# The recurrent mixers: mask inside the minimum, q and k decayed in place, half of each score tile copied, row broadcasts in fp32r parts

## The chip, the cores and the metric

The kernel runs on one core of a Trainium2 chip. The metric is the device time of one execution in microseconds (us), the median of several runs.

## The reference

Two blocks of transformer-like layers run one after the other over 256 tokens of width 1024, in fp32. The first has four layers, each a mixer and a SwiGLU feed-forward with layer norms: gated DeltaNet (gdn), hgrn2, gla, gated DeltaNet again. The second has two layers ("four") with four small mixers side by side. The change concerns the causal part of three mixers:

```python
def chunk_gla(q, k, v, g):            # hgrn2 (8 heads of 128) and gla (4 heads of 128 keys, 256 values)
    G = jnp.cumsum(g, axis=-2)        # g <= 0, one decay per token and key channel
    rel = jnp.exp(jnp.where(incl, G_c[..., :, None, :] - G_c[..., None, :, :], -jnp.inf))
    a = jnp.einsum('bhcd,bhsd,bhcsd->bhcs', q_c, k_c, rel)
    ...
def chunk_gated_delta_rule(q, k, v, beta, g):   # gdn, 8 heads
    decay = jnp.exp(jnp.where(incl, G[..., :, None] - G[..., None, :], -jnp.inf))
    L = jnp.where(strict, jnp.einsum('bhncd,bhnsd->bhncs', kb, k) * decay, 0.0)
    sol = lax.linalg.triangular_solve(L + jnp.eye(CHUNK, dtype=F32), rhs, ...)
    a_qk = jnp.einsum('bhncd,bhnsd->bhncs', q, k) * decay
    ...
```

The Mamba-like mixer of the "four" layers masks its decay in the same way: `where(tri, exp(where(tri, seg, 0)), 0)`.

## The kernel before, in words

Five engines run programs of their own and meet at semaphores. The weights stream from HBM into a ring of six slots; DVE or ACT casts a slot to its fp32r high part (`w_hi`), DVE and POOL subtract it from the slot to get the low part (`w_lo`), and PE multiplies high by high, high by low and low by high. `units_in(kind)` lists the slots of a mixer's input projection. In the projection of hgrn and gla, DVE's `split` of the next slots is placed by hand between the mixer's own vector work, by calls of `due(n)`.

**hgrn and gla** (`gla` on each engine). The 256 tokens are halved again and again: at level `lv` a block of `2 << lv` tokens has a first half (keys) and a second half (queries). For each of eight levels POOL subtracts from the cumulated log decay its value at the block's middle (`differences`, L1361), ACT takes the exponential of both halves, DVE multiplies k and q by it into a fresh copy (`decayed`, L1888 `inv<-yb,ct` and `inv<-pj,ct`), PE multiplies all tokens of each 128-token tile with each other (L980, or L988 for the last level), and DVE copies what the level's mask selects into the score matrix `at`, which lies in the tile `mats` (`masked`, COPY_PREDICATED, L2358). PE also runs filler matmuls (`stay_awake`, L574) at levels 0 and 1. Then PE multiplies the scores with the values (L818, L819).

**gdn**. For each of eight heads PE broadcasts the two rows (cumulated decay and beta) over the partitions (L849, `ident` against `rows`, fp32), DVE forms the clipped difference in `dec` (L1894) and `kbeta`, ACT takes the exponential, POOL multiplies by the causal mask `incl` (L1396), and DVE multiplies both score tiles by it (`scores`, `mats<-bank,dec`). Then a triangular inverse is built by doubling, over six levels and four groups of matrices: POOL masks (L1402), DVE takes identity minus that (`XT` of level 0, `inv<-ident,ct`), PE transposes (L923), forms `cx` (L867) and corrects (L935, at level 6 L937), ACT copies `cx` and transposes out of PSUM, DVE subtracts.

**four**. DVE forms the same clipped difference for four heads, ACT the exponential, DVE multiplies by `incl` and then by the scores (L1888); the rotation of q and k stands behind it on DVE.

## Time and profile before

| what | value |
|---|---|
| median of 3 runs | 2405.71 us (2405.37 to 2406.33) |
| the profiled execution's own time | 2406.07 us |
| its span in the trace | 2404.4 us |
| PE, DVE, ACT, POOL busy | 94%, 65%, 38%, 20% of the span |
| mean granted TensorE clock | 0.959 of full speed |

Times in the trace are counted from the span's start. The span leaves 1.7 us of the execution's time outside. The recurrent mixers stand at about 125 to 235 us (gdn), 555 to 617 (hgrn), 923 to 962 (gla) and 1295 to 1405 (gdn again); the "four" mixers lie behind 1620.

### The profile page before, as it was taken

Reading aid. Unit: us, or ns where it says so; the run is one execution under the profiler, and the core shown is the slowest. Engines: PE = TensorE matmul, PEld = TensorE weight load, DVE = VectorE, ACT = ScalarE, POOL = GpSimd, SP = SyncE. Lnnn points to the kernel's source line nnn. Section 1 sums busy time; section 2 is a strip of 40 time slices with the busy share of each in tenths; the row PEclk is TensorE's granted clock in tenths of the full one; section 3 lists DMA queues with packets and bytes.
Section 4 is the critical chain, followed back from the end, with each engine's and each line's share of the span. In section 5 each row is a group of like instructions: output and inputs, shape, how many; then the busy total and the mean of one; then the engine's idle time right before and its main releaser. Section 6 shows DMA issues by size and latency. Waiting matters only on the chain.

```text
span 2404.4 us, 33475 instructions
## 1 busy us (share of the span) xinstructions
PE 2261.9 (94%) x13233; PEld 1949.9 (81%) x13233; DVE 1572.1 (65%) x1914; ACT 902.7 (38%) x1193; POOL 469.1 (20%) x259
## 2 busy tenths in 40 slices
PE   8999999997999988999899999998889999978999
PEld 7988788887788778788798878877658997847998
DVE  7843754798854567844695275456467887457787
ACT  3324344333344413444413334442453333254332
POOL 6643000156000044000063500004120001320000
PEclk9989999999999999999999899999879999969999
DMA  7500565551265542565462026555204554503552
GB/s 219 163 31 19 175 193 187 165 181 46 98 216 184 170 142 86 176 192 185 132 187 94 1 88 219 185 159 160 72 27 165 181 188 131 166 0 100 190 187 94
DMA packets 265598, 333.69 MB, mean 139 GB/s; under 512 B 16492, under 2 KB 228593, under 8 KB 265473
## 3 DMA queue, kind: packets, MB, share of 16 engines
q1 hardware_dynamic: 265473, 331.93, 43.1%
q8 instruction: 90, 1.47, 0.3%
q14 instruction: 35, 0.29, 0.0%
HBM read 330.84 MB, written 1.05 MB: 138 GB/s over the span
## 4 chain that ended last, share of the span: by engine, by line
PE 82%; DVE 10%; ACT 4%; issue 3%; POOL 2%; DVEq 0%; POOLq 0%; ACTq 0%
PE bank L530 41%; PE bank L502 26%; DVE inv L1888 3%; PE bank L867 2%; PE bank L935 2%; PE bank L574 1%; PE bank L564 1%; DVE w_hi L1932 1%; ACT stat L1409 1%; PE bank L923 1%; DVE mats L2358 1%; PE bank L721 1%; PE bank L849 1%; PE bank L1070 1%; ACT xh L1409 1%
## 5 line engine op out<-in xcount | busy, mean ns | idle before, releaser
L1934 DVE TENSOR_TENSOR w_lo<-ring,w_hi 128x2048 fp32r<-128x2048 f32 (+3 forms) x297 | 562.0, 1894 | 328.6 <-ACT w_hi L1455 325.4
L1455 ACT ACTIVATE w_hi<-ring 128x2048 fp32r<-128x2048 f32 x204 | 385.5, 1890 | 463.6 <-PE bank L530 299.2
L1350 POOL TENSOR_TENSOR w_lo<-ring,w_hi 128x1536 fp32r<-128x1536 f32 (+3 forms) x71 | 277.0, 3902 | 1402.3 <-DVE w_hi L1932 1402.3
L530 PE MATMUL bank<-w_lo,xh 128*128 128x512 f32 x992 | 268.2, 392 | 4.2 <-POOL w_lo L1350 4.2
L530 PE MATMUL bank<-w_hi,xh 128*128 128x512 f32 x928 | 251.1, 392 | 11.9 <-ACT xh L1409 7.4
L502 PE MATMUL bank<-xh,w_lo 128*128 128x256 f32 (+2 forms) x1880 | 246.3, 284 | 4.8 <-POOL w_lo L1350 4.7
L530 PE MATMUL bank<-w_hi,xl 128*128 128x512 f32 x928 | 249.0, 390 | 0.0
L502 PE MATMUL bank<-xh,w_hi 128*128 128x256 f32 (+1 forms) x1816 | 242.0, 287 | 4.3 <-DVE w_hi L1932 4.3
L502 PEld LDWEIGHTS bank<-xh,w_lo 128*128 128x128 f32 (+2 forms) x1880 | 232.1, 188 | 8.0 <-issue 5.6
L502 PEld LDWEIGHTS bank<-xh,w_hi 128*128 128x128 f32 (+1 forms) x1816 | 229.3, 192 | 11.3 <-issue 6.5
L502 PE MATMUL bank<-xl,w_hi 128*128 128x256 f32 (+1 forms) x1816 | 236.4, 283 | 0.0
L502 PEld LDWEIGHTS bank<-xl,w_hi 128*128 128x128 f32 (+1 forms) x1816 | 224.9, 190 | 0.7
L530 PEld LDWEIGHTS bank<-w_lo,xh 128*128 128x128 f32 x992 | 185.5, 189 | 43.6 <-issue 6.1
L530 PEld LDWEIGHTS bank<-w_hi,xh 128*128 128x128 f32 x928 | 173.1, 188 | 51.5 <-issue 11.6
L530 PEld LDWEIGHTS bank<-w_hi,xl 128*128 128x128 f32 x928 | 174.8, 188 | 36.8
L1932 DVE CAST w_hi<-ring 128x2048 fp32r<-128x2048 f32 (+2 forms) x93 | 171.0, 1839 | 43.2 <-PE bank L502 23.4
L530 PE MATMUL bank<-w_hi,hid_hi 128*128 128x512 f32 x528 | 169.0, 401 | 8.1 <-DVE hid_lo L1888 8.1
L530 PE MATMUL bank<-w_hi,hid_lo 128*128 128x512 f32 x528 | 165.1, 394 | 0.0
L530 PE MATMUL bank<-w_lo,hid_hi 128*128 128x512 f32 x528 | 164.3, 393 | 0.0
L1409 ACT ACTIVATE yb<-bank 128x256 f32<-128x256 f32 (+3 forms) x146 | 59.0, 404 | 171.4 <-PE bank L530 124.9
L530 PEld LDWEIGHTS bank<-w_lo,hid_hi 128*128 128x128 f32 x528 | 100.2, 190 | 21.9
L530 PEld LDWEIGHTS bank<-w_hi,hid_lo 128*128 128x128 f32 x528 | 100.1, 190 | 21.9
(300 smaller groups left out, 2801.4 us busy)
## 6 DMA issues: line engine op xcount, KB each, us to landing
ring<-in_ffn_w_in_dram SPq DMA_DIRECT2D x264, 512.0 KB, 4.5
ring<-in_ffn_w_down_dram SPq DMA_DIRECT2D x88, 512.0 KB, 4.3
ring<-in_gdn_w_in_dram SPq DMA_DIRECT2D x64, 512.0 KB, 5.1
ring<-in_ffn_w_out_dram SPq DMA_DIRECT2D x44, 512.0 KB, 4.1
ring<-in_w_in_dram SPq DMA_DIRECT2D x36, 512.0 KB, 4.6
ring<-in_hgrn_w_in_dram SPq DMA_DIRECT2D x32, 512.0 KB, 4.6
...
```

The lines of the kernel that those rows point to most:

```text
L502: m = nc.tensor.matmul(cols, *((wk, xk) if tokens == ALL else (xk, wk)), start=(first and step == 0 and k == 0 and (j % 2 == 0)), stop=(la ...
L530: m = nc.tensor.matmul(bank[:, 0:width], xin[:, k0 + k, rows_of], w[:, k, c * width:(c + 1) * width], start=(first and step == 0 and k == ...
L564: m = nc.tensor.transpose(b[:, j * P:(j + 1) * P], src[:, t, c * CHUNK + j * P:c * CHUNK + (j + 1) * P], ident[:, :])
L574: m = nc.tensor.matmul(b[:, 0:T], ones[:, :], incl[:, 0:T], start=True, stop=True)
L867: m = nc.tensor.matmul(b[:, (j % 4) * HALF2:(j % 4 + 1) * HALF2].rearrange("p (n c) -> p n c", c=1 << lv), ct[:, j, :], first_halves(inv[: ...
L935: m = nc.tensor.matmul(b[:, cols], inv[:, 16 + j, :], cx[:, j, :], start=True, stop=True)
L1350: g.tensor_tensor(w_lo[:, unit % RING, part], ring[:, unit % RING, part], high_part(unit)[:, part], ALU.subtract).then_inc(*pool_lo.tick())
L1409: nc.scalar.activation(out_, in_, func, **kw).then_inc(*sig.tick(*key))
L1455: nc.scalar.activation(high_part(u)[:, 0:n], ring[:, u % RING, 0:n], ACT.Copy).then_inc(*act_hi.tick())
L1888: v.tensor_tensor(out_, a, b, op).then_inc(*sig.tick(*key))
L1932: v.tensor_copy(high[:, 0:n], w[:, 0:n]).then_inc(*dve_hi.tick())
L1934: v.tensor_tensor(w_lo[:, u % RING, 0:share], w[:, 0:share], high[:, 0:share], ALU.subtract).then_inc(*dve_lo.tick())
```

## The change

In hgrn and gla the running sum of log decays, POOL's differences and ACT's exponentials go away. The decay itself (`ratio`) is multiplied up pairwise into the decay of blocks of 2, 4, ... tokens (`block_ratio`). q is multiplied once by the decay of its own token (`qd`, which lies in `sq`), and from level to level k and `qd` are multiplied in place: only the half of each block that moves on is touched (`grown`), half of the heads at a time. The masked copy touches only the second half of each block's columns, 64 of each 128. The scores lie in `own` (two 128-token squares for each head) and `across` (the first against the second 128 tokens). The last of the eight levels is a plain copy. The fillers at levels 0 and 1 and the clearing of `at` are dropped. hgrn's scale of q moves into the later norm, and its log of the bounded forget gate is formed as `sigma * (1 - lb) + lb`.

In gdn and four the mask lies in the minimum (`imask` holds 0 or -1e30), so the multiplications by `incl` go. The rows to be broadcast are split into fp32r high and low parts, one matmul of 512 columns for each. The level-0 groups of gdn's inverse are taken in the order 0, 2, 1, 3, the first two between the last heads' scores. At level 6 `cx` is formed for the 64 rows and columns that are not zero. The core of the diff, without the setup of masks and the changed ACT code of the forget gate:

```diff
-                    for j in range(2):
-                        m = nc.tensor.matmul(b[:, j * T:(j + 1) * T], ident[0:8, h:h + 1].to_broadcast([8, P]), rows[0:8, j, :], start=True, stop=True)
+                    for n, part in enumerate((rows_hi, rows_lo)):
+                        m = nc.tensor.matmul(b[:, :], pick[0:8, h:h + 1].to_broadcast([8, P]),
+                                             part[0:8, :, :].rearrange("p a n -> p (a n)"), start=(n == 0), stop=(n == 1))
                     m.then_inc(*pe_gdn.tick("bcast", layer, h))
...
-                for g in range(4):
+                for g in (0, 2, 1, 3):
...
-                            m = nc.tensor.matmul(b[:, (j % 4) * HALF2:(j % 4 + 1) * HALF2].rearrange("p (n c) -> p n c", c=1 << lv),
-                                                 ct[:, j, :], first_halves(inv[:, j, :], lv), start=True, stop=True)
+                            cols_of = slice((j % 4) * HALF2, (j % 4 + 1) * HALF2)
+                            if lv < 6:
+                                m = nc.tensor.matmul(b[:, cols_of].rearrange("p (n c) -> p n c", c=1 << lv),
+                                                     ct[:, j, :], first_halves(inv[:, j, :], lv), start=True, stop=True)
+                            else:
+                                m = nc.tensor.matmul(b[HALF2:HALF, cols_of], ct[0:HALF2, j, HALF2:HALF], inv[0:HALF2, j, 0:HALF2],
+                                                     start=True, stop=True)
...
+                        m = nc.tensor.matmul(b[0:HALF2, cols], cx[HALF2:HALF, j, :], inv[HALF2:HALF, 16 + j, HALF2:HALF], start=True, stop=True)
                 m.then_inc(*pe_gdn.tick("z", layer, lv, g))
...
+                pe.wait_ge(*dve_gla.at("q decayed", layer))
+                for lv in range(8):
+                    for g in range(2):
+                        if lv:
+                            pe.wait_ge(*dve_gla.at("grown", layer, lv - 1, g))
+                        if lv == 7:
+                            b = psum.claim(pe, "level", layer, lv, g)
+                            for j in range(heads // 2):
+                                h = g * heads // 2 + j
+                                m = nc.tensor.matmul(b[:, j * P:(j + 1) * P], k[:, h, 0:HALF], qd[:, h, HALF:T],
+                                                     start=True, stop=True)
+                            m.then_inc(*pe_gla.tick("level", layer, lv, g))
+                            continue
+                        for n in range(heads // 4):
+                            b = psum.claim(pe, "level", layer, lv, g, n)
+                            for j in range(4):
+                                h, t = g * heads // 2 + 2 * n + j // 2, slice((j % 2) * HALF, (j % 2 + 1) * HALF)
+                                m = nc.tensor.matmul(b[:, j * P:(j + 1) * P], k[:, h, t], qd[:, h, t], start=True, stop=True)
+                            m.then_inc(*pe_gla.tick("level", layer, lv, g, n))
...
-                    pe.wait_ge(*dve_gla.at("causal", layer))
+                    pe.wait_ge(*dve_gla.at("causal", layer, g // 2))
...
-                for h in range(8):
-                    pool.wait_ge(*act_gdn.at("decay", layer, h))
-                    d = dec[:, h % 2, :]
-                    g.tensor_tensor(d, d, incl[:, :], ALU.mult).then_inc(*pool_gdn.tick("decay", layer, h))
                 for lv in range(7):
...
-                    dve.wait_ge(*pool_gdn.at("decay", layer, h))
+                    dve.wait_ge(*act_gdn.at("decay", layer, h))
...
+                def first_inverse(g):
+                    dve.wait_ge(*pool_gdn.at("masked", layer, 0, g))
+                    tt(s, inv[:, 16 + 4 * g:16 + 4 * g + 4, :], ident[:, :].rearrange("p (a n) -> p a n", a=1).to_broadcast([P, 4, P]),
+                       ct[:, 4 * g:4 * g + 4, :], ALU.subtract, "XT", layer, 0, g)
...
-                    ts(s, dec[:, h % 2, 0:T], b[:, 0:T], cols[:, 0, h:h + 1], ALU.subtract, 0.0, ALU.min)
-                    ts(s, dec[:, h % 2, T:TRI], b[:, HALF:T], cols[:, 2, h:h + 1], ALU.subtract, 0.0, ALU.min,
-                       "difference", layer, h)
+                    stt(s, dec[:, h % 2, 0:T], b[:, 0:T], cols[:, 0, h:h + 1], imask[:, 0:T], ALU.subtract, ALU.min)
+                    stt(s, dec[:, h % 2, T:TRI], b[:, HALF:T], cols[:, 2, h:h + 1], imask[:, T:TRI], ALU.subtract, ALU.min,
+                        "difference", layer, h)
                     tt(s, sq[:, h, :], pj[:, 8 + h, :], b[:, T:2 * T], ALU.mult, "kbeta", layer, h)
                     psum.release(s, "bcast", layer, h)
                     if h:
                         scores(h - 1)
+                    if h >= 6:
...
-                    dve.wait_ge(*pool_gdn.at("masked", layer, 0, g))
-                    tt(s, inv[:, 16 + 4 * g:16 + 4 * g + 4, :], ident[:, :].rearrange("p (a n) -> p a n", a=1).to_broadcast([P, 4, P]),
-                       ct[:, 4 * g:4 * g + 4, :], ALU.subtract, "XT", layer, 0, g)
+                for g in (1, 3):
+                    first_inverse(g)
...
+                    tt(s, flat(ct), ratio, f, ALU.subtract, "log k", layer)
+                    due(2)
+                    dve.wait_ge(*s.now())
+                    dve.wait_ge(*act_gla.at("sigma", layer))
                     for h in range(8):
-                        ts(s, sq[:, h, :], decayed_sum[:, h * T:(h + 1) * T], lbs[:, 5, h:h + 1], ALU.add, lbs[:, 4, h:h + 1], ALU.subtract,
-                           "f against bound", layer)
-                    due()
+                        ts(s, ratio[:, h * T:(h + 1) * T], sq[:, h, :], lbs[:, 5, h:h + 1], ALU.mult, lbs[:, 4, h:h + 1], ALU.add)
+                dve.wait_ge(*act_gla.at("sigma", layer))
+                dve.wait_ge(*act_gla.at("k", layer))
+                due()
+                for lv in range(6):
+                    w = block_ratio(lv, heads)
                     dve.wait_ge(*s.now())
-                    for h in range(8):
-                        ts(s, decayed_sum[:, h * T:(h + 1) * T], decayed_sum[:, h * T:(h + 1) * T], lbs[:, 5, h:h + 1], ALU.add, lbs[:, 4, h:h + 1], ALU.max)
-                    due(2)
...
-                dve.wait_ge(*s.now())
-                for h in range(heads):
-                    scan(s, pj[:, 8 + h, :], decayed_sum[:, h * T:(h + 1) * T], "cumulated", layer)
-                    if h == 3:
+                    tt(s, block_ratio(lv + 1, heads).rearrange("p h n two -> p h (n two)"), w[:, :, :, 0], w[:, :, :, 1], ALU.mult)
+                    if lv < 2:
                         due()
-                due(2)
                 dve.wait_ge(*act_proj.at("q", layer, 6 if kind == "hgrn" else 2))
-                if kind == "hgrn":
-                    ts(s, flat(q), flat(q), 128.0 ** -0.5, ALU.mult)
-                s.name_also("qk", layer)
+                tt(s, flat(qd)[:, 0:n], flat(q), ratio[:, 0:n], ALU.mult, "q decayed", layer)
...
+                def grown(lv, g):
+                    of, w = slice(g * hg, (g + 1) * hg), block_ratio(lv, heads)
+                    if lv < 6:
+                        kg, qg, wk, wq = kk[:, of, :], qd[:, of, :], w[:, of, :, 1], w[:, of, :, 0]
+                    else:
+                        kg, qg, wk, wq = kk[:, of, 0:HALF], qd[:, of, HALF:T], w[:, of, 0:1, 1], w[:, of, 1:2, 0]
+                    for x, by, which in ((kg, wk, 0), (qg, wq, 1)):
+                        x = halves(x, lv, which)
+                        tt(s, x, x, by.rearrange("p h (n a) -> p h n a", a=1).to_broadcast(list(x.shape)), ALU.mult, "grown", layer, lv, g)
...
+                def masked(lv, g):
+                    c = 1 << lv
+                    m = halves(level[:, lv:lv + 1, :].bitcast(U32), lv, 1).to_broadcast([P, 4, HALF2 // c, c])
+                    for n in range(hg // 2):
+                        h0 = g * hg + 2 * n
+                        to = own[:, h0:h0 + 2, :, :].rearrange("p h t n -> p (h t) n")
+                        scores = psum.bank("level", layer, lv, g, n)[:, :].rearrange("p (a n) -> p a n", a=4)
+                        v.copy_predicated(halves(to, lv, 1), m, halves(scores, lv, 1)).then_inc(*s.tick("masked", layer, lv, g))
+                        psum.release(s, "level", layer, lv, g, n)
...
+                for lv in range(7):
+                    for g in range(2):
+                        dve.wait_ge(*pe_gla.at("level", layer, lv, g, hg // 2 - 1))
+                        if lv:
+                            dve.wait_ge(*s.at("masked", layer, lv - 1, g))
+                        else:
+                            dve.wait_ge(*s.now())
+                        grown(lv, g)
+                        masked(lv, g)
...
+                        stt(s, at[:, h, 0:T], b[:, j * T:(j + 1) * T], cols[:, 0, h:h + 1], imask[:, 0:T], ALU.subtract, ALU.min)
+                        stt(s, at[:, h, T:TRI], b[:, j * T + HALF:(j + 1) * T], cols[:, 2, h:h + 1], imask[:, T:TRI], ALU.subtract, ALU.min,
+                            "difference", layer, h)
...
-                    tt(s, at[:, h, :], at[:, h, :], incl[:, :], ALU.mult)
-                    dve.wait_ge(*s.now())
                     tt(s, at2[:, 4 + h, :], psum.bank("bc", layer, h // 2)[:, 0:TRI], at[:, h, :], ALU.mult, "causal", layer, 3)
```

**DVE in hgrn's levels, before.** `inv` takes k (`yb`) and q (`pj`) times the decays (`ct` or `sq`); `mats` is the score tile. Levels 0 and 1:

```order
L1888 TENSOR_TENSOR inv<-yb,ct 128x1024
L1888 TENSOR_TENSOR inv<-pj,ct 128x1024
L2369 MEMSET mats 128x3072
L2358 COPY_PREDICATED mats<-ident,bank 128x2x2x128 x4
L1888 TENSOR_TENSOR inv<-yb,sq 128x512x2
L1888 TENSOR_TENSOR inv<-pj,sq 128x512x2
L2358 COPY_PREDICATED mats<-level,bank 128x2x2x128 x4
```

**The same place after.** `yb` is k and `sq` is the decayed q, both in place; `inv` holds the block decays; the second `yb`, `sq` pair is the other half of the heads at level 0:

```order
L1887 TENSOR_TENSOR mats<-bank,ident 128x512 x4
L1887 TENSOR_TENSOR yb<-yb,inv 128x512
L1887 TENSOR_TENSOR sq<-sq,inv 128x512
L2360 COPY_PREDICATED mats<-level,bank 128x256 x2
L1887 TENSOR_TENSOR yb<-yb,inv 128x512
L1887 TENSOR_TENSOR sq<-sq,inv 128x512
L2360 COPY_PREDICATED mats<-level,bank 128x256 x2
```

The long multiplications have become twice as many of half the length, into their own operand; each masked copy moves 256 elements in a partition in place of 512, and the memset is gone.

**DVE at the end of gdn's scores, before** (`mats` are the two score tiles, `inv<-ident,ct` the level-0 inverses):

```order
L1894 TENSOR_SCALAR dec<-bank,cols 128x256
L1894 TENSOR_SCALAR dec<-bank,cols 128x128
L1888 TENSOR_TENSOR sq<-pj,bank 128x256
L1888 TENSOR_TENSOR mats<-bank,dec 128x384 x2
L1894 TENSOR_SCALAR dec<-bank,cols 128x256
L1894 TENSOR_SCALAR dec<-bank,cols 128x128
L1888 TENSOR_TENSOR sq<-pj,bank 128x256
L1888 TENSOR_TENSOR mats<-bank,dec 128x384 x4
L1888 TENSOR_TENSOR inv<-ident,ct 128x512 x4
```

**After:**

```order
L1897 SCALAR_TENSOR_TENSOR dec<-bank,cols,imask 128x256
L1897 SCALAR_TENSOR_TENSOR dec<-bank,cols,imask 128x128
L1887 TENSOR_TENSOR sq<-pj,bank 128x256
L1887 TENSOR_TENSOR mats<-bank,dec 128x384 x2
L1887 TENSOR_TENSOR inv<-ident,ct 128x512
L1897 SCALAR_TENSOR_TENSOR dec<-bank,cols,imask 128x256
L1897 SCALAR_TENSOR_TENSOR dec<-bank,cols,imask 128x128
L1887 TENSOR_TENSOR sq<-pj,bank 128x256
L1887 TENSOR_TENSOR mats<-bank,dec 128x384 x2
L1887 TENSOR_TENSOR inv<-ident,ct 128x512
L1887 TENSOR_TENSOR mats<-bank,dec 128x384 x2
L1887 TENSOR_TENSOR inv<-ident,ct 128x512 x2
```

Two of the four level-0 inverses have moved ahead of the last heads' scores.

**DVE in hgrn's projection, from the log decay on, before** (each CAST with its `w_lo` is one slot of weights):

```order
L1932 CAST w_hi<-ring 128x2048
L1934 TENSOR_TENSOR w_lo<-ring,w_hi 128x512
L1932 CAST w_hi<-ring 128x2048
L1934 TENSOR_TENSOR w_lo<-ring,w_hi 128x512
L1888 TENSOR_TENSOR inv<-inv,ct 128x2048
L1903 SCALAR_TENSOR_TENSOR pj<-const,inv 128x256 x4
L1932 CAST w_hi<-ring 128x2048
L1934 TENSOR_TENSOR w_lo<-ring,w_hi 128x512
L1903 SCALAR_TENSOR_TENSOR pj<-const,inv 128x256 x4
L1932 CAST w_hi<-ring 128x2048
L1934 TENSOR_TENSOR w_lo<-ring,w_hi 128x512
L1892 TENSOR_SCALAR pj<-pj 128x2048
```

**After:**

```order
L1887 TENSOR_TENSOR ct<-inv 128x1024
L1931 CAST w_hi<-ring 128x2048
L1933 TENSOR_TENSOR w_lo<-ring,w_hi 128x512
L1887 TENSOR_TENSOR ct<-ct 128x512
L1931 CAST w_hi<-ring 128x2048
L1933 TENSOR_TENSOR w_lo<-ring,w_hi 128x512
L1887 TENSOR_TENSOR ct<-ct 128x256
L1887 TENSOR_TENSOR ct<-ct 128x128
L1887 TENSOR_TENSOR ct<-ct 128x64
L1887 TENSOR_TENSOR ct<-ct 128x32
L1887 TENSOR_TENSOR sq<-pj,inv 128x2048
L1931 CAST w_hi<-ring 128x2048
```

Eight of the sixteen multiplications by the bounds (ahead of these rows), the eight scans, the add and the scaling of q are gone; short products of decays and one long product (`sq<-pj,inv`) stand ahead of the last slot's cast.

## Rows read from the trace of the kernel before

**Rows 1.** The page: busy time, share of the span and instructions of each engine

```profile
PE 2261.9 (94%) x13233; PEld 1949.9 (81%) x13233; DVE 1572.1 (65%) x1914; ACT 902.7 (38%) x1193; POOL 469.1 (20%) x259
```

**Rows 2.** Stretch of hgrn's levels: busy PE, PEld, DVE, ACT, POOL; granted clock; DMA

```profile
559.70:609.70 50.00, 37.49 (x260) 35.18 (x258) 49.14 (x52) 14.23 (x14) 23.31 (x7) 0.90 0.01 2
```

**Rows 3.** Timeline of DVE, hgrn's last levels: start, duration, operation, count

```profile
597.76 2.27 DVE L1888 TENSOR_TENSOR inv<-yb,ct 128x1024 f32<-128x1024 f32 x1
601.20 2.55 DVE L2358 COPY_PREDICATED mats<-level,bank 128x512 f32<-128x512 uint32 x4
603.66 1.20 DVE L1888 TENSOR_TENSOR inv<-yb,sq 128x1024 f32<-128x1024 f32 x1
```

**Rows 4.** Timeline of PE, hgrn: scores of one pass, values

```profile
554.90 3.74 PE L980 MATMUL bank<-pj,yb 128*128 128x128 f32 x32
609.91 0.67 PE L818 MATMUL bank<-mats,vb 128*128 128x256 f32 x2 [1.50 <-DVE mats L2374]
```

**Rows 5.** Timeline of gla: PE's first scores and values, DVE's last level

```profile
922.74 1.95 PE L980 MATMUL bank<-pj 128*128 128x128 f32 x16
950.43 1.28 DVE L1888 TENSOR_TENSOR inv<-pj,sq 128x512 f32<-128x512 f32 x2
953.80 0.67 PE L818 MATMUL bank<-mats,vb 128*128 128x256 f32 x2 [0.88 <-DVE mats L2374]
```

**Rows 6.** Timeline around the two projections' PE waits (idle time in brackets)

```profile
531.99 5.60 DVE L1888 TENSOR_TENSOR inv<-inv,ct 128x2048 f32<-128x2048 f32 x1
541.33 2.15 PE L502 MATMUL bank<-xh,w_hi 128*128 128x256 f32 x16 [3.02 <-DVE w_hi L1932]
895.96 1.17 PE L530 MATMUL bank<-w_lo,xh 128*128 128x512 f32 x4 [2.02 <-POOL w_lo L1350]
```

**Rows 7.** Timeline of one head of gdn's scores, PE and DVE

```profile
143.27 1.12 PE L849 MATMUL bank<-rows,ident 8*128 8x256 f32 x4
144.44 0.74 DVE L1894 TENSOR_SCALAR dec<-bank,cols 128x256 f32<-128x256 f32 x2 [0.50 <-PE bank L849]
145.42 1.08 DVE L1888 TENSOR_TENSOR mats<-bank,dec 128x384 f32<-128x384 f32 x2
145.83 1.12 PE L849 MATMUL bank<-rows,ident 8*128 8x256 f32 x4
```

**Rows 8.** Timeline from gdn's last scores to the first `cx`

```profile
151.90 14.10 POOL L1402 TENSOR_TENSOR ct<-mats,level 128x512 f32<-128x512 f32 x10
151.97 1.02 DVE L1888 TENSOR_TENSOR mats<-bank,dec 128x384 f32<-128x384 f32 x2 [0.35 <-POOL dec L1396]
153.21 6.76 DVE L1888 TENSOR_TENSOR inv<-ident,ct 128x512 f32<-128x512 f32 x4 [0.21 <-POOL ct L1402]
156.76 0.63 PE L923 MATMUL bank<-ident,inv 128*128 128x128 f32 x4 [1.05 <-DVE inv L1888]
161.00 3.51 PE L867 MATMUL bank<-inv,ct 128*128 128x64 f32 x16
```

**Rows 9.** Stretches of gdn's inverse: length, PE busy, granted clock

```profile
161.00:196.00 35.00, 34.67 (x241) 0.76 0.00 1
196.00:214.10 18.10, 17.77 (x161) 1.00 0.00 1
1330.50:1390.60 60.10, 59.45 (x466) 0.85 0.00 1
```

**Rows 10.** Timeline of PE in level 6: both matmul forms

```profile
216.05 0.68 PE L937 MATMUL bank<-inv,yb 128*64 128x64 f32 x8
216.66 1.10 PE L867 MATMUL bank<-inv,ct 128*128 128x64 f32 x8
```

**Rows 11.** The first "four" layer: DVE's mask multiplications, PE's wait, clock behind

```profile
1729.36 1.27 DVE L1888 TENSOR_TENSOR mats<-mats,incl 128x384 f32<-128x384 f32 x1
1738.24 0.76 PE L1092 MATMUL bank<-pj 64*128 64x128 f32 x2 [4.34 <-DVE pj L1888]
1734.30:1775.20 40.90, 28.43 (x71) 15.74 (x72) 22.79 (x54) 22.25 (x68) 13.05 (x12) 0.50 0.00 1
```

More of the change, by code:

```diff
@@ L51 @@
 CHAIN = [("gdn", 0), ("hgrn", 0), ("gla", 0), ("gdn", 1), ("four", 0), ("four", 1)]
-FILL = {"mixed": 9, "gdn": 5, "c2": 7, "kbeta": 5, "masked": 4, "level": 6, "softmax": 2}
+FILL = {"mixed": 9, "gdn": 5, "c2": 7, "kbeta": 5, "masked": 4, "softmax": 2}
 CHUNK = 4 * P
@@ L573, in stay_awake @@
                 for _ in range(n):
-                    m = nc.tensor.matmul(b[:, 0:T], ones[:, :], incl[:, 0:T], start=True, stop=True)
+                    m = nc.tensor.matmul(b[:, 0:T], ones[:, :], strict[:, 0:T], start=True, stop=True)
                 m.then_inc(*pe_filler.tick())
@@ L1311, in _ @@
                 fill(const[:, c:c + 1], v)
-            for ap in (blk64, incl, strict, later):
+            for ap in (blk64, strict, later):
                 fill(ap[:, :], 1.0)
-            for ap in (rot64, rot96, amask):
+            for ap in (rot64, rot96, amask, imask):
                 fill(ap[:, :], 0.0)
@@ L1725, in gla_decays @@
                     act.wait_ge(*dve_gla.at("bounds", layer))
-                    run(s, flat(lbs[:, 4:6]), flat(lbs[:, 4:6]), ACT.Ln, "log bounds", layer)
+                    run(s, lbs[:, 7, :], lbs[:, 7, :], ACT.Ln, "log bounds", layer)
                 else:
@@ L2363, in gla @@
[L2363 to L2377 removed]
+                hg = heads // 2
@@ new lines, in diagonal @@
+                def diagonal():
+                    m = ident[:, :].rearrange("p (a n) -> p a n", a=1).to_broadcast([P, 4, P])
+                    for g in range(hg):
+                        dve.wait_ge(*pe_gla.at("diagonal", layer, g))
+                        tt(s, own[:, 2 * g:2 * g + 2, :, :].rearrange("p h t n -> p (h t) n"),
+                           psum.bank("diagonal", layer, g)[:, :].rearrange("p (a n) -> p a n", a=4), m, ALU.mult, "diagonal", layer)
+                        psum.release(s, "diagonal", layer, g)
```

172 lines of the change are left out of this document (56 added, 116 removed).

## The prediction

> **What bounds the kernel now.** The page's first part says that PE is busy for 94% of the span [rows 1]. Most of that is fp32 projection and feed-forward work that the change does not touch. An edit to DVE, ACT or POOL can therefore pay only where PE waits for them or runs at the lower clock, so I read the mixers' stretches one by one, and in each what PE's next work waited for.
>
> In hgrn's levels the table of stretches shows DVE busy 49.14 of 50.0 us and PE 37.49 [rows 2]. A level takes DVE two long multiplications and four masked copies; from one to the next it is 603.66 less 597.76, 5.90 us [rows 3]. One level costs PE 3.74 us [rows 4]. So DVE sets the pace. The end of the projection is 554.8 us, where the first scores start, and the values start at 609.9: 55.1 us [rows 4]. gla is the same with half the heads: 922.7 to 953.8, 31.1 us [rows 5].
>
> In gdn's scores DVE waits 0.50 us for a broadcast in each head [rows 7] and PE is the pace. Behind the scores, POOL's masks (14.10/10 = 1.41 us each) and DVE's level-0 inverses (6.76/4 = 1.69 us each) go side by side, PE waits for each of them, and the first `cx` starts at 161.0 [rows 8]. From then on PE is busy nearly all the time, but at a mean granted clock of 0.76 until 196, that is partly at 1.2 in place of 2.4 GHz; the two levels from 196.0 to 214.1 ran at full clock, 18.1/2 = 9.05 us each [rows 9]. Before the clock fell PE had done short transposes with waits of about 1 us between them [rows 8].
>
> In "four" PE waits 4.34 us for DVE's rotation, which stands behind the mask multiplications [rows 11].
>
> **hgrn's levels.** The long multiplication took 2.27 us beside POOL and 1.20 alone [rows 3]; POOL has no work there any more. A multiplication of 512 elements, alone, is 1.28/2 = 0.64 us and steps at 0.655 [rows 5]. A masked copy of 512 steps at 2.55/4 = 0.64 [rows 3]. One of 256 has no row. From 1024 to 512 the multiplication fell by 1.20 - 0.64 = 0.56, or 1.1 ns an element, so 256 elements less are 0.27 and the copy is 0.38. The bounds are 0.32, half the old price, and 0.64, if strided reads save nothing. I take 0.38, since the strided multiplications before cost no more than others. A level is then 4 x 0.655 + 4 x 0.38 = 4.14 us. Six of them and the seventh with halved multiplications (4 x 0.39 + 4 x 0.38 = 3.1) are 27.9. PE's 3.74 fits beneath 4.14: one half of the heads costs it 1.87 us, while DVE has 2.8 us of other work before it needs the result. Ahead of that stand PE's diagonal scores (3.74) and the first half of level 0 (1.9), behind it one plain copy (0.65): the values start 34.5 us after the projection, not 55.1. **-20.6.** With copies at 0.64 it would be -13.3, with 0.32 -22.
>
> The Trainium skill, page "VectorE: DVE Perf Modes", section on the TRN2 errata, speaks against cutting operations in two: a fixed cost for each instruction, and (N + 151)/0.96 ns for an fp32 two-tensor operation. By it a level would be 4 x 0.69 + 4 x 0.42 = 4.44 us (an estimate), and hgrn's gain 2 us smaller. The row's 1.28 for two agrees with the single duration nearly, but successive operations overlap.
>
> **gla's levels.** A level is 4 multiplications of 256 (0.39) and 2 copies (0.38): 2.3 us; PE needs 1.95, its reply to one half 0.95 plus a hand-over of some 0.1 inside 1.5. Six, a seventh of 1.8, 3.0 ahead, 0.4 behind: the values start after 19.0 us in place of 31.1. **-12.1.** With copies at 0.64: -8.5.
>
> The fillers that go are 2.8 us of PE each, under DVE's time before. Their cover was for the clock; PE will be busy 90% (hgrn) and 80% (gla) of a level, against 3.74/5.9 = 63% before, so I cost their absence at nothing. If the cover is missed see the rivals.
>
> **The projections.** DVE's stretch in hgrn loses 8 bound multiplications, the 5.60 us addition [rows 6], scans and scaling, and gets products of under 3 us and one of 2048 elements (5.6 us beside POOL [rows 6], 2.3 alone). PE waits there three times, 6.2 us together, the longest 3.02 [rows 6]. Walking DVE's new order against PE's 5.8 us a slot, with a product held until POOL's current `w_lo` ends, the two waits in the middle go, and a wait of some 2.5 us stays before the last slot, whose cast stands behind the long product. **-3.8**, which is the 6.2 less the 2.5 that stays (from -1 to -7.7, where all PE idle goes, gaps between matmuls too). In gla a cast comes 1.7 us earlier and shortens PE's 2.02 us [rows 6]: **-1.7**; the larger wait ahead of it, for the gates, stays.
>
> **gdn, each of two.** (a) Broadcasts: PE's 1.06 us a head becomes two fp32r matmuls of 512 columns, of which the projection does four in 1.17 us [rows 6]: 0.6. The head then costs PE 2.0 and DVE about 2.2 (144.44 to 145.42 + 1.08, with what queues between heads) in place of the cadence 2.56 [rows 7]: 6 x 0.33 + 1.0 for the first two = 3.0; two inverses now stand in this stretch, +1.3; POOL's mask (0.35 on the last head [rows 8]) goes. -2.0. A subtraction with `imask` in place of 0 costs the same 0.74 for 384 elements. (b) Behind the last `lt` (152.5, the first of the two at 151.97 [rows 8]) `cx` came 8.5 us later. Now two POOL masks (2.8), an inverse (1.7) and a transpose (0.7) stand there: 5.4. -3.1. (c) Clock. The first three levels took 35.0 us; at the full clock's 9.05 they are 27.2 [rows 9]. PE's waits shrink to one of about 1 us, so I take it that the clock stays high: -7.8. (d) In level 6 the 64-wide form of 8 steps at 0.61 (216.05 to 216.66), the 128-wide at 1.03 [rows 10]: 4 x 0.42, of which 1.5 counts. Sum -14.4. The second gdn has the same rows to 0.1 us and a clock of 0.85 over its stage [rows 9]: **-28.8** for both.
>
> **four, each of two.** The first mask multiplication took 1.27 us, others 0.55 to 1.2, four of them some 3.3 us in steps [rows 11], all on the path to PE's wait of 4.34. **-3.3 each, -6.6.** Lower bound nothing, if POOL's rotation is late next; that ended ahead of DVE.
>
> The two-step split of gdn's rows adds 1 us of DVE at 40 us, where `rows` is not needed before 127. SP's queue keeps its order; no weight is waited for in these stretches.
>
> **Sum**: 20.6 + 12.1 + 3.8 + 1.7 + 28.8 + 6.6 = 73.6. The profiled execution took 2406.07 us (span 2404.4 and 1.7 around it), 0.4 above the median, so 2332.5, and 2332 against the median.
>
> **Rivals.**
> 1. The clock falls in gdn all the same, because PE's short waits remain (the transposes of groups 1 and 3) : +7.8 each, 2348. For it: the clock fell before on waits of only 1 us. Against: there were four of them in 8 us, now one. Chance 0.20.
> 2. The levels run slower than DVE's sum: copies at 0.64 give 7.3 + 3.6 = 11 us back, 2343; or PE, without fillers, falls to 1.2 GHz and needs 7.4 us a level in hgrn and 3.7 in gla, +22 and +10, 2364. Against the latter: 63% busy brought a mean clock of 0.90 [rows 2], no more. 0.12.
> 3. More is gained: all PE idle of hgrn's projection (4 us more), and in "four" the clock, which is 0.50 from 1734 to 1775 with PE 28.4 us busy [rows 11], comes back for part of it once the 4.34 us wait is gone. A third of the 28.4/2 us that it costs, twice, is 9: 2319. 0.13.
> 4. Slower than before. The in-place forms, with one decay repeated over a block and runs as short as one element, cost DVE more than any row here. The levels hold 56 + 42 = 98 such operations on the path. At 73.6/98 = 0.75 us more for each, above twice their price, the gain is gone; at 0.85 us more each it is 2332 + 98 x 0.85 = 2415. Against it: the level-0 operations of before stepped over two elements and cost the same 1.2. 0.03.
>
> Forecast 0.52, its own range 2323 to 2343. Less than 0.2% (4.8 us) either way is what a measurement of this kernel can't tell from no change. Faster 0.96, same 0.01, slower 0.03. The range takes in rivals 1 and 3 and the copies' bound: 2312 to 2356.
>
> **What would show it.** hgrn's values start about 34 us behind its last projection matmul, gla's 19; DVE without pause between them, masked copies near 0.4 us; PE's clock at full there. In gdn `cx` starts 5 to 6 us after the last `lt`, the clock stays high and the stage ends 14 us earlier. In "four" PE's wait is 1 us. Wrong would be: PE waits of over 1 us in each level, a clock of 0.5 behind gdn's scores, or copies of 0.6.

## The result, and the profile after

Medians of four executions each: 2405.77 us before (2405.37 to 2406.33), 2329.80 us after (2327.10 to 2331.76). The ratio is 0.9679, 95% interval 0.9664 to 0.9694: faster by 76 us, 3.2%. The forecast was 2332. The profiled execution took 2331.76 us (span 2330.1, mean clock 0.972).

The sum hit, but not each of its terms. Where the time went is read from PE's timeline. A stage lasts from PE's first matmul behind a mixer's input projection to the end of its last one ahead of the mixer's output projection. A gap is what lies between two stages: output projection, feed-forward and the next input projection, with PE's wait of 0.1 to 0.6 us just ahead of the output projection. Lengths in the two profiles, in us:

| stage or gap | before | after | difference | forecast |
|---|---|---|---|---|
| gdn, first | 114.7 | 99.0 | -15.7 | -14.4 |
| gap with hgrn's projection | 315.2 | 312.1 | -3.1 | -3.8 |
| hgrn | 68.4 | 47.5 | -20.9 | -20.6 |
| gap with gla's projection | 299.4 | 297.5 | -1.9 | -1.7 |
| gla | 44.1 | 31.5 | -12.6 | -12.1 |
| gdn, second | 115.3 | 106.8 | -8.5 | -14.4 |
| four, first | 90.8 | 85.7 | -5.1 | -3.3 |
| four, second | 90.4 | 83.3 | -7.1 | -3.3 |

The three other gaps differ by less than 0.1, by +0.7 and by -0.7 us and cancel; the stretches ahead of the first mixer and behind the last one grew by 0.5 and 0.1. In all that is the 74.3 us between the two spans. In the first "four" PE's wait ahead of the output projection also fell, from 0.59 to 0.09 us, which stands in the gap. First the page of the kernel after, its first part, which answers to [rows 1]:

```profile
PE 2213.6 (95%) x13185; PEld 1915.0 (82%) x13185; DVE 1527.5 (66%) x1923; ACT 873.9 (38%) x1160; POOL 407.5 (17%) x227
```

PE's busy time fell by 48 us though its matmuls hardly got fewer: part of it is work that no longer runs at half clock, part the fillers that went.

**hgrn's levels.** The table of stretches and, under it, the timelines of DVE and PE in the kernel after, answering to [rows 2 to 4]:

```profile
546.00:571.00 25.00, 23.78 (x196) 22.86 (x197) 24.88 (x54) 0.00 (x0) 0.00 (x0) 1.00 0.00 1
```

```profile
542.17 0.69 DVE L1887 TENSOR_TENSOR yb<-yb,inv 128x512 f32<-128x512 f32 x1 [1.10 <-PE bank L1009]
...
547.11 0.73 DVE L1887 TENSOR_TENSOR yb<-yb,ct 128x512 f32<-128x512 f32 x1
...
548.36 1.32 DVE L2360 COPY_PREDICATED mats<-level,bank 128x256 f32<-128x256 uint32 x2
549.46 0.73 DVE L1887 TENSOR_TENSOR yb<-yb,ct 128x512 f32<-128x512 f32 x1
...
551.81 0.72 DVE L1887 TENSOR_TENSOR yb<-yb,ct 128x512 f32<-128x512 f32 x1
...
559.31 0.68 DVE L1887 TENSOR_TENSOR yb<-yb,ct 128x512 f32<-128x512 f32 x1
...
560.51 0.76 DVE L2360 COPY_PREDICATED mats<-level,bank 128x256 f32<-128x256 uint32 x2
561.17 0.68 DVE L1887 TENSOR_TENSOR yb<-yb,ct 128x512 f32<-128x512 f32 x1
...
566.78 0.41 DVE L1887 TENSOR_TENSOR yb<-yb,ct 128x256 f32<-128x256 f32 x1
...
569.68 1.36 DVE L2376 COPY mats<-bank 128x512 f32<-128x512 f32 x2
```

```profile
536.61 3.74 PE L990 MATMUL bank<-pj,yb 128*128 128x128 f32 x32
...
553.18 15.12 PE L1009 MATMUL bank<-sq,yb 128*128 128x128 f32 x128 [0.29 <-DVE sq L1887]
...
570.51 0.46 PE L1018 MATMUL bank<-mats,vb 128*128 128x128 f32 x2 [0.20 <-DVE mats L2376]
```

The values start 570.51 - 536.61 = 33.9 us behind the projection (34.5 forecast; 609.91 - 554.90 = 55.0 before). Two copies take 549.46 - 548.36 = 1.10 us at level 1, where the runs are two elements long, and 561.17 - 560.51 = 0.66 at later levels, where they are four or longer: 0.55 and 0.33 each, on either side of the 0.38 I took. Half a level is then 561.17 - 559.31 = 1.86 us of DVE against PE's 1.87, and PE runs the 128 matmuls of levels 3 to 6 without a pause: there the two engines are level, and the clock is 1.00 with no filler.

**gla and the projections.** PE's timeline of the kernel after, for [rows 5, 6]:

```profile
529.29 2.96 PE L513 MATMUL bank<-xh,w_hi 128*128 128x256 f32 x16 [2.29 <-DVE w_hi L1931]
532.05 2.80 PE L513 MATMUL bank<-xl,w_hi 128*128 128x256 f32 x16
```

```profile
881.58 1.95 PE L990 MATMUL bank<-pj 128*128 128x128 f32 x16
...
899.99 0.46 PE L1018 MATMUL bank<-mats,vb 128*128 128x128 f32 x2
```

gla's values start after 18.4 us (19.0 forecast, 31.1 before). In hgrn's projection one long wait of PE is left, 2.29 us, ahead of the last slot (some 2.5 forecast). Behind it PE is slow for a while: the two rows of sixteen matmuls take 2.96 and 2.80 us. With the same wait in e4 below they take 2.15 and 2.08:

```profile
528.93 2.15 PE L513 MATMUL bank<-xh,w_hi 128*128 128x256 f32 x16 [2.29 <-DVE w_hi L1933]
```

The granted clock in that stretch (529.3 to 534.7) is 0.68. This dip costs 1.3 us: the gap with hgrn's projection is 311.9 to 312.1 us in every profile that has it (after, e2, e3, f1, f3, f4, g3) and 310.8 in those that have the wait and not the dip (e1, e4, f2, g1).

**gdn.** PE's timeline from the last filler to the first `cx`, first and second gdn of the kernel after, and the stretches around them (for [rows 7 to 9]):

```profile
149.96 1.89 PE L585 MATMUL bank<-strict,ones 128*128 128x256 f32 x8
...
153.76 0.63 PE L940 MATMUL bank<-ident,inv 128*128 128x128 f32 x4 [0.76 <-DVE inv L1887]
155.43 0.63 PE L940 MATMUL bank<-ident,inv 128*128 128x128 f32 x4 [1.05 <-DVE inv L1887]
155.90 1.90 PE L881 MATMUL bank<-inv,ct 128*128 128x64 f32 x16
...
1269.08 0.63 PE L940 MATMUL bank<-ident,inv 128*128 128x128 f32 x4 [0.77 <-DVE inv L1887]
1270.75 0.90 PE L940 MATMUL bank<-ident,inv 128*128 128x128 f32 x4 [1.05 <-DVE inv L1887]
1271.44 3.52 PE L881 MATMUL bank<-inv,ct 128*128 128x64 f32 x16
```

```profile
156.00:170.00 14.00, 13.84 (x127) 13.63 (x126) 2.49 (x6) 5.68 (x12) 11.51 (x10) 1.00 0.00 1
1271.30:1285.00 13.70, 13.70 (x68) 13.70 (x66) 1.26 (x3) 2.73 (x6) 7.87 (x7) 0.50 0.00 0
```

Both layers have the same waits, 0.76 and 1.05 us. Behind the first the clock stayed at 1.00 (2.4 GHz) and sixteen `cx` took 1.90 us; behind the second it fell to 0.50 (1.2 GHz) and they took 3.52. Work at half clock, for some 17 us, is the 7.8 us between 99.0 and 106.8.

**four.** PE's timeline of the first "four" after, for [rows 11]:

```profile
1674.44 0.46 PE L1115 MATMUL bank<-pj 64*128 64x128 f32 x2 [1.96 <-DVE pj L1887]
...
1675.26 1.10 PE L1093 MATMUL bank<-xn,rot 96*96 96x512 f32 x2
```

The wait for the rotation is 1.96 in place of 4.34 us (about 1 was forecast), and the rotations behind it, 2.02 us each at half clock before, take 1.10.

### The profile page after: what moved, and what is told of

Its sections match the earlier page's. It is cut to its first block, busy times and chain, and to the rows that moved or that the text cites. A ratio compares the mean times of both kernels' runs of the same rounds, so it can differ in the third digit from the quotient of the medians.

```text
span 2330.1 us, 33338 instructions
## 1 busy us (share of the span) xinstructions
PE 2213.6 (95%) x13185; PEld 1915.0 (82%) x13185; DVE 1527.5 (66%) x1923; ACT 873.9 (38%) x1160; POOL 407.5 (17%) x227
## 3 DMA queue, kind: packets, MB, share of 16 engines
HBM read 330.84 MB, written 1.05 MB: 142 GB/s over the span
## 4 chain that ended last, share of the span: by engine, by line
PE 85%; DVE 9%; ACT 3%; issue 2%; POOL 1%; DVEq 0%; POOLq 0%; ACTq 0%
PE bank L541 42%; PE bank L513 27%; PE bank L952 2%; PE bank L881 2%; PE bank L585 1%; PE bank L1009 1%; DVE w_hi L1931 1%; PE bank L575 1%; PE bank L732 1%; PE bank L940 1%; ACT w_hi L1459 1%; ACT mats L1413 1%; ACT xh L1413 1%; DVE w_lo L1933 1%; PE bank L838 1%
## 5 line engine op out<-in xcount | busy, mean ns | idle before, releaser
L1931 DVE CAST w_hi<-ring 128x2048 fp32r<-128x2048 f32 (+2 forms) x93 | 160.2, 1723 | 43.9 <-PE bank L513 22.9
L1413 ACT ACTIVATE yb<-bank 128x256 f32<-128x256 f32 (+4 forms) x146 | 59.0, 404 | 162.1 <-PE bank L541 124.9
```

Source lines behind the costliest of these rows:

```text
L1413: nc.scalar.activation(out_, in_, func, **kw).then_inc(*sig.tick(*key))
L1931: v.tensor_copy(high[:, 0:n], w[:, 0:n]).then_inc(*dve_hi.tick())
```

## The experiments

The lengths below are those of the table above, read from each kernel's own profile. The six stages, in us (gdn, hgrn, gla, gdn, four, four):

| kernel | stages | time |
|---|---|---|
| before | 114.7, 68.4, 44.1, 115.3, 90.8, 90.4 | 2405.8 |
| after | 99.0, 47.5, 31.5, 106.8, 85.7, 83.3 | 2329.8 |
| e1 levels alone | 114.5, 47.5, 31.5, 114.9, 90.0, 90.0 | 2366.4 |
| e2 order of groups back | 108.0, 47.5, 31.5, 109.1, 92.9, 84.3 | 2347.9 |
| e3 four's mask back | 106.8, 47.5, 31.5, 106.8, 87.7, 90.0 | 2352.4 |
| e4 idle matmuls in gdn | 99.0, 47.5, 31.5, 99.1, 89.2, 83.4 | 2324.9 |
| f1 = e4, fp32 broadcasts | 101.9, 47.5, 31.5, 101.9, 84.6, 84.3 | 2326.5 |
| f2 = e4, full copies | 99.0, 53.1, 34.1, 99.0, 88.1, 83.4 | 2333.0 |
| f3 = e4, full level 6 | 101.4, 47.5, 31.5, 101.4, 88.2, 84.3 | 2330.6 |
| f4 no filler in gdn | 106.8, 47.5, 31.5, 106.8, 86.9, 85.3 | 2339.4 |
| g1 = e4, idle matmuls in four | 99.0, 47.5, 31.5, 99.1, 86.9, 82.2 | 2319.0 |
| g2 = e4, last cast earlier | 99.0, 47.5, 31.5, 99.0, 88.3, 84.3 | 2324.6 |
| g3 = e4, four's mask back | 99.0, 47.5, 31.5, 99.0, 94.7, 90.0 | 2341.4 |
| g4 = g1 and g2 | 99.0, 47.5, 31.5, 99.0, 85.4, 82.2 | 2318.1 |

The times of after and of e1 to e4 are medians of four executions, g4's of five; f1 to g3 had one execution each, so of these only the stage that was edited is read. hgrn and gla repeat to 0.1 us. gdn takes one of two lengths, 7.8 us apart. With the code of the kernel after, the first "four" took from 84.6 to 92.9 us, the second from 83.3 to 85.3.

**e1, the levels alone.** gdn and four as before, hgrn and gla changed:

```diff
-stt(s, dec[:, h % 2, 0:T], b[:, 0:T], cols[:, 0, h:h + 1], imask[:, 0:T], ALU.subtract, ALU.min)
+ts(s, dec[:, h % 2, 0:T], b[:, 0:T], cols[:, 0, h:h + 1], ALU.subtract, 0.0, ALU.min)
...
+g.tensor_tensor(d, d, incl[:, :], ALU.mult).then_inc(*pool_gdn.tick("decay", layer, h))
...
```

> The changed hgrn and gla with gdn and four as they were before (masks multiplied in, fp32 broadcasts, inverse groups 0, 1, 2, 3 behind the scores, full level 6). If the parts add up, this gains what the two profiles show in hgrn and gla: 3.1 + 20.9 + 1.7 + 12.6 = 38.3 us, so 2367.5 us, within 2 us. If instead the shorter levels gave gdn or four a different clock (or the reverse), the gain differs from 38 by more than 4 us.

2366.38 us: 40.0 below its median of before (2406.36), where the two profiles' four lines for hgrn and gla add up to 38.5, and the two "four" layers were 1.2 us shorter here. The parts add; the levels did not touch the clock elsewhere. Its ratio is 0.9825, interval 0.9788 to 0.9863.

**e2, the order of the groups.**

```diff
-for g in (0, 2, 1, 3): gdn_transpose(layer, 0, g)
+for g in range(4): gdn_transpose(layer, 0, g)
...
-if h >= 6: first_inverse(2 * (h - 6))
```

> The changed kernel with the level-0 groups of gdn taken 0, 1, 2, 3 and all four inverses behind the last head's scores. My theory: the order is worth 3 us in each gdn (PE again waits for four mask and inverse pairs, the first cx comes 8 to 9 us behind the last scores), and these waits let the granted clock fall to 0.5 behind them in both gdn layers, 7.5 us each at most: the first gdn loses 10 us, the second 3, in all some 2343 us. Rival: the clock falls by chance and not by these waits; then the first gdn stays at full clock and the loss is 6 us, 2336.

2347.92 us, ratio 0.9765 (0.9709 to 0.9821). My theory said 2343, its rival 2336. PE's timeline of this kernel, where the waits are four again:

```profile
151.36 0.63 PE L940 MATMUL bank<-ident,inv 128*128 128x128 f32 x4 [0.32 <-DVE inv L1887]
153.03 0.63 PE L940 MATMUL bank<-ident,inv 128*128 128x128 f32 x4 [1.05 <-DVE inv L1887]
154.70 0.63 PE L940 MATMUL bank<-ident,inv 128*128 128x128 f32 x4 [1.04 <-DVE inv L1887]
156.38 1.09 PE L940 MATMUL bank<-ident,inv 128*128 128x128 f32 x4 [1.05 <-DVE inv L1887]
157.26 3.09 PE L881 MATMUL bank<-inv,ct 128*128 128x64 f32 x14
```

The stage started at 125.2, so `cx` starts at 32.0 us in it, against 155.90 - 125.5 = 30.4 after: the order is worth 1.6 us, less than the 3 I expected, since the two inverses no longer stretch the scores. The clock fell in both gdn layers, and the first took 8.9 us more than in the kernel after. That the order is what keeps the clock is not shown by this: it fell in one of the two layers of the kernel after as well, and in both of e3, which has the order of the kernel after. Another 7.2 us of the loss are the first "four", whose code this edit leaves alone.

**e3, four's mask multiplications.**

```diff
+tt(s, at[:, h, :], at[:, h, :], incl[:, :], ALU.mult)
+dve.wait_ge(*s.now())
```

> The changed kernel with four's multiplications of the decays by the 0/1 mask put back (four of 384 elements on DVE, on top of the mask in the minimum). Theory A, the price is DVE's alone: 3.3 us in each of the two, 2336.4. Theory B, the two profiles' 5.1 and 7.1 us: the longer wait of PE for the rotation also costs the clock behind it, so 12 us, 2342. Theory C, the ACT chain behind it bounds: under 1 us.

2352.41 us, but from 2334.37 to 2354.12, interval of the ratio 0.9691 to 0.9802. The stage table shows why: gdn, whose code is that of the kernel after, took 106.8 us twice in the profiled execution. 2350.83 less 2 x 7.8 is 2335.2, near the fastest one. As a measure of four it did not decide; g3 repeats it with gdn's clock held.

**e4, idle matmuls in gdn's waits.**

```diff
 for g in (0, 2, 1, 3):
+    if g % 2: stay_awake((g + 1) // 2)
     gdn_transpose(layer, 0, g)
```

> The changed kernel with idle matmuls of PE (strict by ones) ahead of gdn's transposes of groups 1 and 3: one before the first, two before the second, 0.47 us each at full clock, within the waits of 0.77 and 1.05 us. If the short waits are what lets the clock fall in the second gdn, its clock stays at 1.00 and it ends 7.5 us earlier: 2322 to 2324. Rival: the clock falls there for another reason; then 2330, or 1 us more where an idle matmul at half clock holds up the next transpose.

2324.85 us (2322.18 to 2331.77), ratio 0.9656 (0.9615 to 0.9697). PE's timeline of this kernel:

```profile
152.51 0.60 PE L585 MATMUL bank<-strict,ones 128*128 128x256 f32 x2
153.44 0.63 PE L942 MATMUL bank<-ident,inv 128*128 128x128 f32 x4 [0.33 <-DVE inv L1889]
153.90 1.03 PE L585 MATMUL bank<-strict,ones 128*128 128x256 f32 x4
155.12 0.63 PE L942 MATMUL bank<-ident,inv 128*128 128x128 f32 x4 [0.19 <-DVE inv L1889]
155.58 1.90 PE L883 MATMUL bank<-inv,ct 128*128 128x64 f32 x16
```

The waits shrink to 0.33 and 0.19 us, `cx` starts no later (30.4 us into the stage), and both layers take 99.1 us. The total shows less of it: the median is 5.0 us below that of the kernel after, where the second gdn gained 7.8, the first "four" was 3.5 us longer here, and the intervals of the two ratios overlap. The finding rests on the stages.

**f4, the opposite:** the existing filler ahead of the transposes taken out.

```diff
-stay_awake(FILL["masked"])
```

> The changed kernel without the four idle matmuls between gdn's last scores and its first transposes (PE then waits about 1.9 us more there and does no less of the stage's work). If short waits behind the scores are what lets the clock fall, both gdn layers now fall to 0.5 for some 14 us and take 106 to 108 us in place of 99.0 and 106.8. Rival: the fall is chance, independent of PE's waits: one or none falls.

PE's timeline of this kernel:

```profile
153.99 0.63 PE L939 MATMUL bank<-ident,inv 128*128 128x128 f32 x4 [2.76 <-DVE inv L1886]
155.66 0.84 PE L939 MATMUL bank<-ident,inv 128*128 128x128 f32 x4 [1.04 <-DVE inv L1886]
156.29 3.52 PE L880 MATMUL bank<-inv,ct 128*128 128x64 f32 x16
```

`cx` starts 30.6 us into the stage, 0.2 later than in the kernel after, and yet both layers took 106.8. Over all profiles: with the waits filled (e4, f1 to f3, g1 to g4) 16 of 16 gdn layers kept the clock; with the waits of the kernel after (its own profile and e3) 1 of 4; with longer or more ones (before, e1, e2, f4) 0 of 8. So PE's waits there do decide. With those of the kernel after both outcomes come.

**f1, fp32 broadcasts.**

```diff
-for n, part in enumerate((rows_hi, rows_lo)):
...
+for j in range(2):
+    m = nc.tensor.matmul(b[:, j * T:(j + 1) * T], ident[0:8, h:h + 1].to_broadcast([8, P]), rows[0:8, j, :], start=True, stop=True)
```

> The kernel with the three idle matmuls in gdn, and in it the fp32 broadcasts put back (two fp32 matmuls of 256 columns a head and one copy of the rows). PE paces the scores at 2.15 us a head and the fp32 form costs it 1.06 us in place of 0.65: theory A says 2.56 a head again, so 8 x 0.41 = 3.2 us in each gdn, the stages 102.2 in place of 99.0. Rival B, DVE paces the heads (its work is 2.15 too) and PE's cost is hidden: under 1 us.

101.9 in both, +2.9 us: theory A, PE paces the scores.

**f2, full copies in the levels.**

```diff
-m = halves(level[:, lv:lv + 1, :].bitcast(U32), lv, 1).to_broadcast([P, 4, HALF2 // c, c])
+m = level[:, lv:lv + 1, :].bitcast(U32).to_broadcast([P, 4, P])
...
-v.copy_predicated(halves(to, lv, 1), m, halves(scores, lv, 1))
+v.copy_predicated(to, m, scores)
```

> The kernel with the three idle matmuls in gdn, and in it the masked copies of hgrn and gla over all 128 columns of a tile (512 elements) in place of the 64 that change. At 0.64 us a copy, against 0.33 measured (0.50 to 0.54 at levels 0 and 1), DVE sets the pace of hgrn's levels at 4.98 us again where PE needs 3.74: hgrn +6.5 us (54 in place of 47.5), gla +3.6 (35 in place of 31.5). Rival: a strided copy costs what its runs cost, and the full copy without strides is cheaper than 0.64: under 5 us together.

hgrn 53.1 (+5.6), gla 34.1 (+2.6). DVE's timeline of this kernel at a late level:

```profile
566.29 1.33 DVE L2362 COPY_PREDICATED mats<-level,bank 128x512 f32<-128x512 uint32 x2
567.51 0.68 DVE L1889 TENSOR_TENSOR yb<-yb,ct 128x512 f32<-128x512 f32 x1
```

Two full copies step by 567.51 - 566.29 = 1.22, 0.61 each, not 0.64, and at levels 0 and 1 they cost only 0.06 us more than the strided ones: hence 8.2 us together and not the 10 expected. The halved copies are a quarter of what the levels gained (8.2 of 33.5).

**f3, level 6 in full.**

```diff
-m = nc.tensor.matmul(b[0:HALF2, cols], cx[HALF2:HALF, j, :], inv[HALF2:HALF, 16 + j, HALF2:HALF], start=True, stop=True)
+m = nc.tensor.matmul(b[0:HALF2, cols], cx[:, j, :], inv[:, 16 + j, HALF2:HALF], start=True, stop=True)
...
```

> The kernel with the three idle matmuls in gdn, and in it level 6 of gdn's inverse in full (cx of 128 rows, the correction over 128). Forecast of the term: 1.5 us in each gdn, 100.5 in place of 99.0. Rival: PE is not the pace in the last level, so nothing.

101.4 in both: +2.4 us, not 1.5. PE's timeline of level 6, first in this kernel, then in the kernel after:

```profile
201.10 1.90 PE L883 MATMUL bank<-inv,ct 128*128 128x64 f32 x16
202.93 0.68 PE L956 MATMUL bank<-inv,yb 128*64 128x64 f32 x8
```

```profile
201.51 1.14 PE L884 MATMUL bank<-inv,ct 64*64 64x64 f32 x16
...
203.09 0.22 PE L954 MATMUL bank<-inv,yb 64*64 64x64 f32 x1
203.14 0.22 PE L884 MATMUL bank<-inv,ct 64*64 64x64 f32 x1
203.15 0.22 PE L954 MATMUL bank<-inv,yb 64*64 64x64 f32 x1
```

Two things come together. Sixteen `cx` take 1.90 us with 128 rows and 1.14 with 64, so by the starts of the single records one costs 0.112 and 0.058 us; over 32 that is 1.7 us, near my 4 x 0.42. My row's 1.03 and 0.61 for eight also held the change from one form to the other, some 0.14 us each time and six times in the level. These changes go too: the new `cx` reads rows 0 to 63, the correction rows 64 to 127, and where the two alternate, from 202.97 to 203.78, PE starts 24 matmuls 0.035 us apart on average, some pairs within 0.01, against 0.058 in a row of one form. That is the rest of the 2.4.

**g3, four's mask again, with gdn's clock held.** The edit is that of e3, on e4's kernel.

> The kernel with the three idle matmuls in gdn, and in it four's multiplications by the mask put back, so that gdn's clock does not blur it. Theory A, the DVE work alone: 3.3 us more in each four, 86.7 in place of 83.4. Theory B, with PE's longer wait the clock falls behind it and costs some 3 us more: 90, as in the kernel before.

94.7 and 90.0, against 89.2 and 83.4: +5.5 and +6.6, theory B. The first "four" had in both kernels an early stretch of half clock, 10 us into the stage, so the pair can be compared; the second repeats e3's 90.0. PE's timeline and a stretch of the second "four" in this kernel, and PE's timeline of the same place in the kernel after:

```profile
2059.91 0.76 PE L1118 MATMUL bank<-pj 64*128 64x128 f32 x2 [4.33 <-DVE pj L1891]
...
2076.68 0.77 PE L1118 MATMUL bank<-yb 96*128 96x128 f32 x2 [1.96 <-DVE small L2492]
```

```profile
2060.00:2080.00 20.00, 17.98 (x42) 9.05 (x42) 13.77 (x31) 8.77 (x29) 7.07 (x6) 0.59 0.00 0
```

```profile
2053.24 0.46 PE L1115 MATMUL bank<-pj 64*128 64x128 f32 x2 [2.11 <-DVE pj L1887]
...
2067.63 0.77 PE L1115 MATMUL bank<-yb 96*128 96x128 f32 x2 [0.30 <-DVE small L2486]
```

The first score starts 37.0 us into the stage here and 33.0 in the kernel after: 4.0 us are DVE's work, where I had taken 3.3. Behind the 4.33 us wait the scores and rotations run at half clock, and from the first score to the fifth it is 2076.68 - 2059.91 = 16.8 us where the kernel after takes 14.4: 2.4 us more are the clock's.

**g1, idle matmuls in four.**

```diff
+if n == 0: stay_awake(4)                 # ahead of the scores
...
+if n in (0, 2, 4): stay_awake({0: 7, 2: 5, 4: 5}[n])   # ahead of the probabilities
```

> The kernel with the three idle matmuls in gdn, and idle matmuls in four too: four ahead of PE's wait of 2.0 us for the rotation, seven ahead of the first transposed probabilities (wait 4.7 us), five ahead of the third and of the fifth (waits 2.7). If the half clock behind those waits costs PE time on the path, each four ends 2 to 4 us earlier than its 83.4 at best. Rival: the softmax chain of DVE and ACT sets the pace there, PE's speed does not matter, and the stages stay at 83 to 84, or are longer by what idle matmuls at half clock hold up.

82.2 in the second "four", 1.1 less than e4's; the stage's mean granted clock is 0.96, against 0.84. PE's timeline of this kernel:

```profile
2057.44 0.30 PE L1131 MATMUL bank<-ident,mats 128*128 128x128 f32 x1 [1.64 <-ACT mats L1419]
```

The rival is nearer: at full clock PE still waits for the softmax's engines, and its half clock there cost little. This one execution took 7.4 us less than e4's profiled one, but 2.3 of that are the first "four", which wanders, and 2.6 lie behind the last "four", where a later dip of the clock is shorter (3.4 us in place of 6.8). f4, which has none of these idle matmuls in "four", shows the same shorter stretch (223.9 us behind the last stage, here 223.8, in e4 226.4), so I do not put it down to them.

**g2, hgrn's last cast ahead of the long product.**

```diff
+due(len(units_in(kind)))
 tt(s, flat(qd)[:, 0:n], flat(q), ratio[:, 0:n], ALU.mult, "q decayed", layer)
-due(len(units_in(kind)))
```

> The kernel with the three idle matmuls in gdn, and DVE's cast of hgrn's last projection slot moved ahead of the 2048-element product of q (in gla too, where no cast is left there or it is early). PE's wait of 2.29 us for that cast should go, and the product, which nothing needs before the diagonal scores end, stays hidden: hgrn's projection 2.2 us shorter, the rest as it was. Rival: the product then ends too late for the first level, and the same 2 us come back as a wait of PE in the mixer.

The gap with hgrn's projection is 308.7 in place of 310.8 (312.1 with the clock's dip), and hgrn stays 47.5; g4 has 308.6 again. PE's timeline of this kernel shows the slot without its wait:

```profile
527.13 2.15 PE L513 MATMUL bank<-xh,w_hi 128*128 128x256 f32 x16
```

**g4, the three together.**

> The changed kernel with the three edits that won or held: idle matmuls ahead of gdn's transposes of groups 1 and 3, idle matmuls in four's waits, and hgrn's last cast ahead of the long product. The stages measured singly: gdn 99.0 and 99.1, four 82.2 in the second, hgrn's projection 2.1 us shorter: 2319 - 2.1 = 2317 us, ratio to the kernel before 0.9633, where the change alone has 0.9679. Rival: a dip of the clock in the first gdn or four that these idle matmuls do not cover comes in some of the executions, and the median stays above 2321.

2318.09 us (2311.61 to 2319.51), ratio 0.9628 with the interval 0.9604 to 0.9652: 11.7 us below the kernel after, and the interval below its 0.9664. Between the two profiled executions the largest parts are the second gdn (7.8 us), the gap with hgrn's projection (3.5, the wait and the dip behind it) and the stretch behind the last "four" (2.5, not put down to an edit, as said at g1).

## Why the prediction was right, term by term

**The levels, -20.6 and -12.1: right** (-20.9, -12.6), in the mechanism and in the sum. DVE paced them before, and cutting its work paid until PE's 3.74 us a level came up. e1 shows that they add to the rest. The size of the single operations was hit in part by luck. The price of the copy, 0.38, was the middle of two: 0.33 for runs of four elements and more, some 0.55 for runs of one and two; a multiplication steps at 0.60, not 0.655. So levels 0 and 1 took 551.81 - 542.17 = 9.6 us, 1.4 more than forecast, the next four 566.78 - 551.81 = 15.0, 1.6 less, and the seven together 27.5 for 27.9. (The terms that I listed add up to 34.2 and not to the 34.5 that I wrote.) By the fixed cost that the Trainium skill, page "VectorE: DVE Perf Modes", section on the TRN2 errata, gives, a level would have been 4.44 us (an estimate); the trace disagrees: 4.9 and 4.7 at levels 0 and 1, 3.7 behind them. One multiplication of 512 elements has a record of 0.68 us, where that formula of the Trainium skill gives 0.69, but the next starts 0.60 us behind it, and this step is what a level costs: for a row of such operations the measurement decides. Rival 2 did not come: the clock in the levels was 1.00 without a filler.

**The projections, -3.8 and -1.7: right** (-3.1, -1.9). The wait that was forecast to stay is the 2.29 us that g2 took away. What it left out is the clock's dip behind that wait, 1.3 us; without it (e1, e4) the first of the two is -4.4.

**gdn, -14.4 each: right in the first, wrong in the second.** The parts were (a) -2.0, measured 27.2 - 24.5 = -2.7 from the stage's start to the filler behind the scores; (b) -3.1, measured 8.8 - 5.9 = -2.9; (d) -1.5, measured -2.4 (f3), of which the cheaper `cx` are 1.7 and the changes between the forms the rest; (c) the clock, -7.8, which came in the first layer (99.0) and not in the second (106.8). The step that failed is "PE's waits shrink to one of about 1 us": two are left, 0.76 and 1.05 us. A clock of 0.5 behind gdn's scores was on my list of what would show the forecast wrong, and it came in the second layer. My rival 1 gave the fall of the clock 0.20 for both layers together; it holds for one of the two, and e4 and f4 show the waits as its cause. Which layer falls in an execution of the kernel after is open: both had the same PE work and waits.

**four, -3.3 each: right in kind, too small** (-5.1, -7.1). The term counted DVE's four multiplications at 3.3 us, which g3 puts at 4.0 in the second "four", and left out what the shorter wait gives back: the clock behind it, named in rival 3, another 2.4 there. g3 measures the whole as 5.5 and 6.6 us. In the first "four" part of it is lost again to a dip of the clock that falls ahead of the scores.

So the 73.6 forecast and the 74.3 between the two profiled spans agree through two misses: 5.9 us too much for the second gdn, 5.6 too little for four, opposite in sign and both about where the clock falls. That the sum came within some 2 us is therefore luck. The range, which took both in, was the sounder statement.
